# Moving a depthwise convolution wholly to VectorE and spreading it and its norm through the attention heads, with the first modulation computed feature tile by feature tile

## The chip, the cores and the metric

The kernel runs on one core of a Trainium2 chip. The metric is the device time of one execution in microseconds (us). A core has engines that run side by side, each with its own queue of instructions: TensorE (PE, matrix products; its weight loads are listed as PEld), VectorE (DVE), ScalarE (ACT), GpSimd (POOL), and SyncE (SP), which here only issues DMAs. They wait for each other on semaphores.

## What is computed

Two transformer blocks on 256 tokens of 1024 features, all in float32. The first block is the one that the change touches:

```python
m = silu(c) @ w_mod + b_mod                     # 6 vectors of 1024: shift, scale, gate, twice
hx = rms_norm(x, g) * (1 + sc1) + sh1           # and the same for ctx, with c_ctx
q, k, v, u, g = split(hx @ w_in)                # 8 query heads, 2 key/value heads of 128
attn = softmax(q k^T / sqrt(128)) v             # 512 keys: ctx and x; q, k are normed and rotated
a, b = split(u)                                 # 512 + 512
h = depthwise_conv(a * sigmoid(b), 31 taps) + bias
y_b = silu(layer_norm(h)) @ w_conv_out
x = x + g1 * ((sigmoid(g_a) * (attn @ w_attn_out) + sigmoid(g_b) * y_b) @ w_out)
x = x + g2 * conv_glu_ffn(rms_norm(x) * (1 + sc2) + sh2)
```

The second block (two gated FFNs, two kinds of attention, a gated embedding) follows. The modulation vectors sh1 and sc1 are needed ahead of every product with hx; g1, sh2, sc2 and g2 only after the attention.

## The kernel before, in words

**Weights and products.** All weights are streamed once from HBM in chunks of 1 MiB (128 partitions x 2048 floats) into four buffers `raw`, by SP in the order of the list `STREAM`. A chunk of a product is then split in two: ACT rounds it (`whi<-raw`, L1031), DVE takes the rest (`wlo<-raw,whi`, L1386), and PE makes three products for each tile instead of one (`product`). There are four buffers of either half too. The features x are split the same way (`x_hi`, `x_lo`). A product whose stationary operand is x has 512 columns (L573 to L575; stages q, kv, w_out, down), one whose stationary operand is the weight has 256 (L576 to L578; stages u, g, attention out, conv out, up). A 1 MiB chunk of the second kind is 48 products and fills one of PSUM's four banks `acc` (`tiles_stage`). A `tiles_stage` waits for `lo_done`, so for both halves.

**Modulation.** `w_mod` needs no split: PE multiplies its raw chunk k, the rows of feature tile k, by silu(c) (L645, four matmuls of 512 columns in four column groups of the array, `mod_chunk`). Each of the three blocks modA, modB, modC covers 2048 outputs, so all eight chunks have to be summed before any output exists. `mod_turn` (L653) then turns the row into columns, DVE adds the bias (L1453), and for modA DVE and ACT apply it to the transposed features (`x_lo`, `x_hi`).

**Order of the stages** is written out by hand in each engine's block and in `STAGES` (which also gives PSUM banks): modA (8 chunks), q (4), u (4), kv (2), g0, g1, then eight heads, in which the remaining g chunks and modB, modC are placed (`MOD_PER_HEAD` = 1, 1, 2, 2, 2, 2, 3, 3), then attention out (4 chunks), conv out (2), w_out (4) and the FFN. In a head PE runs `scores(h)` (L715), `values(h - 1)` (L736), modulation chunks, a g chunk and `prob_transposes(h)` (L724). DVE finds the negated maximum of the scores (L1552), ACT exponentiates (L1153) and scales (L1157), then copies the transposed probabilities (L1169).

**The convolution** has 31 taps on 4 tiles of 128 channels x 256 tokens. Two channel tiles are done on GpSimd (`conv_taps`, L474 and L475: a multiply and an add of 512 columns for each tap, from the end of the kv stage on), the other two on DVE inside the heads (`conv_tap`, L1544, one instruction for a tap and tile, 8 in a head). The layer norm comes after the last head: `ln_mean` (L763), DVE subtracts (L1586), ACT squares (L1176), `ln_var` (L771) inside the attention out stage, GpSimd's root, `ln_broadcast` (L779), DVE scales (L1613), ACT's silu (L1184) and split (L1188), DVE's `cvt_lo` (L1592). The conv out product comes after attention out, then the merge of the branches (L1598, L1623, L1626, L1629).

## Time and profile before

| | us |
|---|---|
| median of 3 runs | 1117.77 (1116.77 to 1118.16) |
| the profiled execution: time | 1119.8 |
| the profiled execution: span of the trace | 1118.0 |
| PE busy | 1018.6 (91%), 6592 matmuls |
| DVE / ACT / POOL busy | 619.9 (55%) / 504.0 (45%) / 136.4 (12%) |
| DMA | 189.02 MB, 169 GB/s on average; 118498 packets, 95312 of them under 2 KB |
| chain that ended last | PE 78%, DVE 13%, ACT 3%, DMA 3% |

All times below are from the span's start. PE is busy nearly all the time from 333 us on (the FFNs and the second block); the change touches only what comes before, except for the layout of the weights in HBM. PE's busy time counts a matmul from start to end and neighbours overlap, so a stretch of matmuls is better read by the distance of their starts.

### The profile page before, as it was taken

The page shows a single profiled execution, that of the slowest core. Times are in us where ns is not written, and L with a number is a line of the kernel's source. Part 1 is how long each engine was busy: PE and PEld are TensorE (multiplying, and loading weights), DVE is VectorE, ACT ScalarE, POOL GpSimd, SP SyncE. Part 2 cuts the span into 40 slices and gives each one's busy share as a digit, 9 for nine tenths or more (in the row PEclk, how much of TensorE's full clock was granted, in tenths as well). Part 3 has the DMA queues.
Part 4 walks back from the last instruction along what each step waited for, and adds up shares of the span by engine and source line. Part 5 has one row for each costly group of instructions (what it writes and reads, how often), then busy time and mean ns, then how long its engine had stood idle before and what let it go on. Part 6 is the DMA issues. An engine that isn't in the chain of part 4 may idle for free.

```text
span 1118.0 us, 15950 instructions
## 1 busy us (share of the span) xinstructions
PE 1018.6 (91%) x6592; PEld 901.3 (81%) x6592; DVE 619.9 (55%) x686; ACT 504.0 (45%) x628; POOL 136.4 (12%) x157
## 2 busy tenths in 40 slices
PE   4699997689989999997999999979999799999997
PEld 1498775458869999985999998778977599999886
DVE  0585387836787666545554544463345664545445
ACT  2563244335435666432544443347633354444343
POOL 3120699500000000001000000010000100000000
PEclk9699998898989999999899999989975899999999
DMA  9755055376555556463555547534421366554621
GB/s 355 278 166 210 3 194 181 113 264 206 188 169 191 187 174 201 174 203 113 188 178 184 171 143 236 178 123 151 148 79 56 115 188 188 183 183 167 213 81 38
DMA packets 118498, 189.02 MB, mean 169 GB/s; under 512 B 3024, under 2 KB 95312, under 8 KB 115376
## 3 DMA queue, kind: packets, MB, share of 16 engines
q1 hardware_dynamic: 116624, 181.61, 48.2%
q0 software_dynamic: 1136, 4.06, 1.2%
q10 hardware_dynamic: 688, 2.63, 0.6%
q8 instruction: 38, 0.62, 0.2%
q14 instruction: 12, 0.10, 0.0%
HBM read 187.24 MB, written 1.05 MB: 168 GB/s over the span
## 4 chain that ended last, share of the span: by engine, by line
PE 78%; DVE 13%; ACT 3%; DMA 3%; issue 1%; POOL 1%; SPq 0%; DVEq 0%; POOLq 0%; ACTq 0%
PE acc L576 15%; PE acc L577 15%; PE acc L578 15%; PE acc L573 9%; PE acc L575 9%; PE acc L574 9%; DVE XN L1544 4%; DVE wlo L1386 3%; DMA raw<-in_w_mod 2%; ACT whi L1031 1%; PE acc L645 1%; DMA raw<-in_w_attn_out 1%; DVE XN L1400 1%; PE tp L662 1%; ACT FULL L1153 1%
## 5 line engine op out<-in xcount | busy, mean ns | idle before, releaser
L1386 DVE TENSOR_TENSOR wlo<-raw,whi 128x2048 fp32r<-128x2048 f32 x148 | 340.1, 2312 | 221.0 <-ACT whi L1031 220.7
L576 PE MATMUL acc<-x_hi,whi 128*128 128x256 f32 x1376 | 395.0, 287 | 3.8 <-DVE x_lo L1424 2.0
L577 PE MATMUL acc<-x_lo,whi 128*128 128x256 f32 x1376 | 392.7, 285 | 0.0
L578 PE MATMUL acc<-x_hi,wlo 128*128 128x256 f32 x1376 | 392.5, 285 | 0.0
L1031 ACT CAST whi<-raw 128x2048 fp32r<-128x2048 f32 x148 | 280.3, 1910 | 184.5 <-PE acc L575 90.9
L576 PEld LDWEIGHTS acc<-x_hi,whi 128*128 128x128 f32 x1376 | 267.6, 194 | 11.6 <-issue 10.0
L577 PEld LDWEIGHTS acc<-x_lo,whi 128*128 128x128 f32 x1376 | 267.7, 195 | 0.0
L578 PEld LDWEIGHTS acc<-x_hi,wlo 128*128 128x128 f32 x1376 | 267.6, 194 | 0.0
L573 PE MATMUL acc<-whi,h_hi 128*128 128x512 f32 x264 | 103.1, 391 | 0.0
L574 PE MATMUL acc<-wlo,h_hi 128*128 128x512 f32 x264 | 102.7, 389 | 0.0
L575 PE MATMUL acc<-whi,h_lo 128*128 128x512 f32 x264 | 102.7, 389 | 0.0
L573 PE MATMUL acc<-whi,x_hi 128*128 128x512 f32 x176 | 72.3, 411 | 12.3 <-DVE x_lo L1431 5.8
L575 PE MATMUL acc<-whi,x_lo 128*128 128x512 f32 x176 | 71.2, 405 | 0.0
L574 PE MATMUL acc<-wlo,x_hi 128*128 128x512 f32 x176 | 71.1, 404 | 0.0
L574 PEld LDWEIGHTS acc<-wlo,h_hi 128*128 128x128 f32 x264 | 49.6, 188 | 10.5 <-issue 0.2
L573 PEld LDWEIGHTS acc<-whi,h_hi 128*128 128x128 f32 x264 | 49.6, 188 | 10.4 <-issue 0.2
L575 PEld LDWEIGHTS acc<-whi,h_lo 128*128 128x128 f32 x264 | 49.6, 188 | 10.2
L517 POOL TENSOR_SCALAR small<-small 128x1 f32<-128x1 f32 x8 | 3.5, 438 | 423.8 <-ACT XN L1261 399.6
L437 POOL TENSOR_SCALAR small<-small 128x1 f32<-128x1 f32 (+2 forms) x19 | 7.4, 390 | 384.7 <-ACT XN L1250 194.2
L573 PEld LDWEIGHTS acc<-whi,x_hi 128*128 128x128 f32 x176 | 34.8, 198 | 22.0 <-issue 10.0
L1544 DVE SCALAR_TENSOR_TENSOR XN<-conv_x,vt,XN 128x256 f32<-128x256 f32 x60 | 51.6, 930 | 0.0
L645 PE MATMUL acc<-raw,sct 128*32 128x512 f32 x192 | 29.6, 727 | 24.0 <-DMA raw<-in_w_mod 20.9
(238 smaller groups left out, 1118.5 us busy)
## 6 DMA issues: line engine op xcount, KB each, us to landing
raw<-in_w_in SPq DMA_DIRECT2D x30, 1024.0 KB, 5.5
raw<-in_w_mod SPq DMA_DIRECT2D x24, 1024.0 KB, 7.9
raw<-in_w_up SPq DMA_DIRECT2D x22, 1024.0 KB, 5.1
raw<-in_w_ffn_gate SPq DMA_DIRECT2D x22, 1024.0 KB, 5.3
raw<-in_w_ffn_up SPq DMA_DIRECT2D x22, 1024.0 KB, 5.4
raw<-in_w_ffn_down SPq DMA_DIRECT2D x22, 1024.0 KB, 5.0
raw<-in_w_down SPq DMA_DIRECT2D x11, 1024.0 KB, 5.0
raw<-in_w_out SPq DMA_DIRECT2D x8, 1024.0 KB, 5.0
```

Of the source, the lines that this page charges most:

```text
L573: pe.matmul(out, xh, wh, start=start, stop=False)
L574: pe.matmul(out, xh, wl, start=False, stop=False)
L575: return pe.matmul(out, xl, wh, start=False, stop=stop)
L576: pe.matmul(out, wh, xh, start=start, stop=False)
L577: pe.matmul(out, wh, xl, start=False, stop=False)
L578: return pe.matmul(out, wl, xh, start=False, stop=stop)
L645: mm = pe.matmul(acc[32 * b:32 * b + 32, MOD_BANK, :], sct[:, k, :], raw[c % NR][:, b * MW:(b + 1) * MW], start=(k == 0), stop=(k == KD - 1))
L662: mm = pe.transpose(tp[:, k // 2, (k % 2) * T + t * P:(k % 2) * T + (t + 1) * P], source[:, t, k * P:(k + 1) * P], ident)
L1031: act.copy(whi[si_slot][:, :], raw[raw_slot][:, :]).then_inc(s["hi_done"], 1)
L1153: act.activation(half(FULL, t), tp[:, t, :], ACT.Exp, bias=nmax[:, t:t + 1], accum_out=psum_[:, t:t + 1]).then_inc(s["p_exp"], 1)
L1386: dve.tensor_tensor(wlo[slot][:, :], raw[raw_slot][:, :], whi[slot][:, :], ALU.subtract)\
L1544: dve.scalar_tensor_tensor(at, conv_x[:, k, i:i + T], w, at, ALU.mult, ALU.add)\
```

## The change

1. **Modulation A by feature tiles.** `modA` leaves `STREAM`. The host lays its weights out so that chunk k holds, for all 1024 inputs, the shift and the scale of feature tile k. It goes into one of four buffers `early` of its own. `first_mod(k)` makes eight matmuls of 256 columns instead of four of 512, `first_turn(k)` sums the column groups and turns them, DVE's `first_row`, `first_out`, `first_lo` and ACT's `first_hi` finish feature tile k. The q stage now takes chunks of two feature tiles by all 1024 columns, and PE runs `q_tile(k - 2)` between `first_mod(k)` and `first_turn(k)`. x is loaded ahead of everything but the vectors, on SP; only 138 of the 1034 columns of constants are loaded first. The context's norm and transposes move behind the u stage.
2. **Convolution on DVE only**, 124 instructions of 256 columns: 16 after the first half of u, 2, 7, 8 and 12 behind the key units, 17 in each head until done (in head 4). GpSimd's `conv_taps` is gone.
3. **Norm and half the product inside the heads.** `ln_mean` and `ln_var` in head 5, `ln_broadcast`, silu and split in head 6; `convout0` takes the place of a g chunk in head 7, `convout1` follows `values(7)`; attention out comes after, and the merge goes column block by column block with it.
4. **Even heads.** Two modulation chunks and one g chunk in each; g1 moves from ahead of the heads into head 0. In head 0 the modulation chunks come ahead of the scores, in head 4 the g chunk comes ahead of them.
5. **One array `stream`** in HBM: the host packs each chunk as 128 rows of 8 KB, where it was read in pieces of 1, 2 or 4 KB (modulation: 8 KB).

The core of the diff:

```diff
-MOD_PER_HEAD = (1, 1, 2, 2, 2, 2, 3, 3)
-
-
-STAGES = [("modA", KD, 1), ("q", 4, 4), ("u", 4, 4), ("kv", 2, 4), ("g0", 1, 1), ("g1", 1, 1)]
+MOD_PER_HEAD = (2, 2, 2, 2, 2, 2, 2, 2)
...
-    if _h + 2 < NH:
-        STAGES.append((f"g{_h + 2}", 1, 1))
-STAGES.append(("pv7", 0, 1))
+        _turn.append((f"{_block}.{_k}", 1, int(_k == KD - 1)))
+    _big = (f"g{_h + 1}", 1, 1) if _h + 1 < NH else ("convout0", 1, 2)
+
+    STAGES += [_big] + _turn if _h == 4 else _turn + [_big]
+    if _h == 5:
+        STAGES.append(("ln_var", 0, 1))
+STAGES += [("pv7", 0, 1), ("convout1", 1, 2)]
 ROTATE3 = {f"g{_h}" for _h in range(NH)} | {f"pv{_h}" for _h in range(NH)}
-STAGES += [(f"attnout{_j}", 1, 1) for _j in range(4)]
-STAGES += [("convout", 2, 4), ("g1b", 0, 2), ("wout", 4, 4), ("up0", 22, 22), ("down0", 11, 4)]
...
+            def ring(c):
+                slot_free(c)
+                sp.dma_start(raw[c % NR][:, :], stream[c, :, :]).then_inc(landed[c % NR], 16)
+
+            def first_block(k):
+                if k >= 4:
+                    sp.wait_ge(s["moda_ps"], k - 3)
...
+            for t in range(TT):
+                sp.dma_start(X[:, t, :], a["x"][t * P:(t + 1) * P, :]).then_inc(s[f"x_in{t}"], 16)
+            first_block(0)
+            ring(POS["q", 0])
+            first_block(1)
+            first_block(2)
+            ring(POS["q", 1])
+            first_block(3)
+            first_block(4)
+            ring(POS["q", 2])
+            first_block(5)
+            first_block(6)
+            ring(POS["q", 3])
+            first_block(7)
+            ring(POS["u", 0])
+            sp.dma_start(consts[:, C_FIRST:C_END], a["consts"][:, C_FIRST:C_END]).then_inc(s["rest_in"], 16)
+            ring(POS["u", 1])
+            sp.dma_start(CTX, a["ctx"].rearrange("(t p) d -> p t d", p=P)).then_inc(s["ctx_in"], 16)
+            for name, j in STREAM[POS["u", 2]:]:
                 c0 = POS[name, 0]
                 if not name.startswith("up"):
-                    c = POS[name, j]
-                    slot_free(c)
-                    w = src[name][j]
-                    sp.dma_start(raw[c % NR][:, :].rearrange("p (k n) -> p k n", k=w.shape[1]), w)\
-                        .then_inc(landed[c % NR], 16)
+                    ring(POS[name, j])
                     continue
...
-            def conv_taps(k0, k1, first):
-
-                out = conv[:, k0:k1, :]
-                for i in range(first, TAPS):
-                    w = per_channel(vt[:, 1, KC * i + k0:KC * i + k1])
-                    x = conv_x[:, k0:k1, i:i + T]
-                    if i == 0:
-                        chain(pool.tensor_tensor(out, x, w, ALU.mult))
-                        chain(pool.tensor_tensor(out, out, per_channel(vec("conv_dw_b", k1 - k0, k0)), ALU.add))
-                        continue
-                    term = half(XN, i % 2)[:, 0:(k1 - k0) * T].rearrange("p (k n) -> p k n", k=k1 - k0)
-                    chain(pool.tensor_tensor(term, x, w, ALU.mult))
-                    ins = pool.tensor_tensor(out, out, term, ALU.add)
-                    if i < TAPS - 1:
-                        chain(ins)
-                ins.then_inc(s["conv_out"], 1)
-
-            conv_taps(KC - KP, KC, 0)
...
+            def first_mod(k):
+
+                pe.wait_ge(early_in[k % 4], 16 * (k // 4 + 1))
+                if k >= 2:
+                    pe.wait_ge(s["mod_row"], k - 1)
+                for j in range(2):
+                    for b in range(MB):
+                        r = MB * j + b
+                        mm = pe.matmul(tp[32 * b:32 * b + 32, k % 2, 0:T], sct[:, r, :],
+                                       early[k % 4][:, r * T:(r + 1) * T], start=(j == 0), stop=(j == 1))
+                mm.then_inc(s["moda_ps"], 1)
+
+            def first_turn(k):
+
+                pe.wait_ge(s["mod_row"], k + 1)
+                for q in range(2):
+                    mm = pe.matmul(tp[:, 2, 4 * k + 2 * q:4 * k + 2 * q + 2],
+                                   modrow[:, (k % 2) * T + q * P:(k % 2) * T + (q + 1) * P], pick_sum,
+                                   start=True, stop=True)
+                mm.then_inc(s["mod_ps"], 1)
...
+            def q_tile(k):
+
+                chunk_ready(SPLIT["q"] + k // 2)
+                pe.wait_ge(s["x0_lo"], k + 1)
+                if k == 0:
+                    pe.wait_ge(s["xt_in"], 4)
+                w = [r[(SPLIT["q"] + k // 2) % NR][:, :].rearrange("p (k n) -> p k n", k=2) for r in (whi, wlo)]
+                for b in range(2):
+                    for t in range(TT):
+                        mm = product(accb(ACC["q"] + 2 * b + t), xhi[:, k, t * P:(t + 1) * P],
...
+            x_transposes(0)
+            first_mod(0)
+            x_transposes(1)
+            first_turn(0)
+            first_mod(1)
+            first_turn(1)
+            for k in range(2, KD - 1):
+                first_mod(k)
+                q_tile(k - 2)
+                first_turn(k)
+            first_mod(KD - 1)
+            first_turn(KD - 1)
+            q_tile(5)
+            q_tile(6)
+            q_tile(7)
 
             def rope_transposes(u):
...
             for h in range(NH):
+                if h == 0:
+                    mod_chunks(0)
                 scores(h)
                 if h:
                     values(h - 1)
+                if h == 5:
+                    ln_mean()
+                if h == 6:
+                    ln_broadcast()
                 if h == MOD_DONE["modB"] + 1:
                     mod_turn("modB")
-                for _, block, k in [m for m in MOD_AT if m[0] == h]:
-                    mod_chunk(block, k, POS[f"{block}.{k}", 0])
-                if h + 2 < NH:
-                    tiles_stage(SPLIT[f"g{h + 2}"], ACC[f"g{h + 2}"])
+                    tiles_stage(SPLIT[f"g{h + 1}"], ACC[f"g{h + 1}"])
+                    mod_chunks(h)
+                elif h + 1 < NH:
+                    if h:
+                        mod_chunks(h)
+                    tiles_stage(SPLIT[f"g{h + 1}"], ACC[f"g{h + 1}"])
+                else:
+                    mod_chunks(h)
+                    conv_products(0)
+                if h == 5:
+                    ln_var()
                 prob_transposes(h)
+            mod_turn("modC")
             values(NH - 1)
-            mod_turn("modC")
-
-
-            sq = QT[:, 0:4, :]
...
+                if h == 5:
+                    act.wait_ge(s["ln_c"], 1)
+                    act.activation(QT[:, 0:4, :], conv, ACT.Square).then_inc(s["ln_sq"], 1)
+                if h == 6:
+                    act.wait_ge(s["ln_n"], 1)
+                    for k in range(KC):
+                        ins = act.activation(QT[:, k, :], conv[:, k, :], ACT.Silu, scale=vec("conv_ln_g", 1, k),
+                                             bias=vec("conv_ln_b", 1, k))
+                    ins.then_inc(s["ln_y"], 1)
+                    act.wait_ge(s["ln_y"], 1)
+                    act.copy(cvt_hi[:, :, :], QT[:, 0:4, :]).then_inc(s["ln_hi"], 1)
+                if h == 7:
...
+            def first_row(k):
+
+                dve.wait_ge(s["moda_ps"], k + 1)
+                dve.tensor_copy(modrow[:, (k % 2) * T:(k % 2 + 1) * T], tp[:, k % 2, 0:T]).then_inc(s["mod_row"], 1)
...
+            def first_lo(k):
+
+                dve.wait_ge(s["x0_hi"], k + 1)
+                dve.wait_ge(s["affine1"], k + 1)
+                dve.scalar_tensor_tensor(FULL[:, k, :], FULL[:, k, :], gainA[:, 0, k:k + 1], xhi[:, k, :], ALU.mult,
+                                         ALU.subtract).then_inc(s["shift_dve"], 1)
+                n_shift[0] += 1
+                dve.wait_ge(s["shift_dve"], n_shift[0])
+                dve.tensor_scalar(xlo[:, k, :], FULL[:, k, :], modv[:, k, 0:1], None, ALU.add).then_inc(s["x0_lo"], 1)
+
...
+            def conv_taps(count):
+
+                for n in range(n_tap[0], min(n_tap[0] + count, TAPS * KC)):
+                    pair, i, k = n // (2 * TAPS), n % (2 * TAPS) // 2, n % 2
...
+                        dve.wait_ge(s["conv_dve"], n - 1)
+                        dve.scalar_tensor_tensor(at, conv_x[:, k, i:i + T], w, at, ALU.mult, ALU.add)\
+                            .then_inc(s["conv_dve"], 1)
+                n_tap[0] = min(n_tap[0] + count, TAPS * KC)
+
...
+                if h == 6:
                     dve.wait_ge(s["ln_r"], 1)
                     for t in range(TT):
                         ins = dve.tensor_scalar(half(XN, 0)[:, t * P:(t + 1) * P], ident, lnv[:, t:t + 1], -1.0,
                                                 ALU.mult, ALU.mult)
                     ins.then_inc(s["ln_diag"], 1)
-                elif j == 1:
-                    dve.wait_ge(s["ln_bc"], 1)
-                    dve.tensor_tensor(cent, cent, over_tiles(tp[:, 2, 0:T]), ALU.mult).then_inc(s["ln_n"], 1)
-            splits_to(SPLIT["convout"] + 2)
-            splits_to(SPLIT["wout"] + 2)
-
-            dve.wait_ge(s["g_sig"], 2)
-            dve.wait_ge(s["ya_done"], 4)
+                conv_taps(3)
+                for t in range(TT):
+                    dve.wait_ge(s["p_exp"], TT * h + t + 1)
+                    dve.reciprocal(prec[:, t:t + 1], psum_[:, t:t + 1]).then_inc(s["p_rec"], 1)
+
+                if h:
+                    pv_lo(h - 1)
+                if h == MOD_DONE["modB"] + 1:
+                    mod_out("modB")
+                if h == 5:
+                    bank_ready(ACC["ln_mean"])
+                    dve.tensor_tensor(conv, conv, over_tiles(accb(ACC["ln_mean"])[:, 0:T]), ALU.subtract)\
+                        .then_inc(s["ln_c"], 1)
+                conv_taps(6)
+                splits_to(SPLIT["g2"] + h + 1)
+                conv_taps(8)
+                if h == MOD_DONE["modB"]:
+                    mod_row("modB")
+                if h == 5:
+                    bank_ready(ACC["ln_var"])
+                    dve.tensor_copy(lnv, accb(ACC["ln_var"])[:, 0:TT]).then_inc(s["ln_ve"], 1)
+                if h == 6:
+                    bank_ready(ACC["ln_bc"])
+                    dve.wait_ge(s["ln_c"], 1)
+                    dve.tensor_tensor(conv, conv, over_tiles(accb(ACC["ln_bc"])[:, 0:T]), ALU.mult)\
...
+    stream = np.empty((len(STREAM), P, CH), np.float32)
+    for c, (name, j) in enumerate(STREAM):
+        w, r, k, c0, n = SOURCE[name][j]
+        stream[c] = arrays[w][r * P:(r + k) * P, c0:c0 + n].reshape(k, P, n).transpose(1, 0, 2).reshape(P, CH)
+    first = arrays["w_mod"][:, 0:2 * D].reshape(KD, P, 2, KD, P).transpose(3, 1, 0, 2, 4)
+    arrays["early"] = np.ascontiguousarray(first).reshape(KD, P, CH)
```

How the order moves. PE at the start of the program, before (L645 is `mod_chunk`, L662 the transposes of x, L653 `mod_turn`, then the products of q):

```order
L645 MATMUL acc<-raw,sct 32x512 x16
L662 MATMUL tp<-consts,XN 128x128 x16
L645 MATMUL acc<-raw,sct 32x512 x16
L653 MATMUL acc<-consts,modrow 128x8 x4
L573 MATMUL acc<-whi,x_hi 128x512
L574 MATMUL acc<-wlo,x_hi 128x512
L575 MATMUL acc<-whi,x_lo 128x512
L573 MATMUL acc<-whi,x_hi 128x512
```

and of the change (L723 the transposes of x, L706 `first_mod`, L714 `first_turn`, L594 to L596 the products of q):

```order
L723 MATMUL acc<-consts,XN 128x128 x8
L706 MATMUL tp<-early,sct 32x256 x8
L723 MATMUL acc<-consts,XN 128x128 x8
L714 MATMUL tp<-consts,modrow 128x2 x2
L706 MATMUL tp<-early,sct 32x256 x8
L714 MATMUL tp<-consts,modrow 128x2 x2
L706 MATMUL tp<-early,sct 32x256 x8
L594 MATMUL acc<-whi,x_hi 128x512
L595 MATMUL acc<-wlo,x_hi 128x512
L596 MATMUL acc<-whi,x_lo 128x512
```

The first q product now comes after three modulation chunks instead of after eight, and after both transposes of x; another modulation chunk and its turn follow each twelve products.

DVE in one head (head 2), before (L1552 maximum, L1556 reciprocal, L1527 `pv_lo`, L1386 split, L1544 convolution):

```order
L1552 TENSOR_REDUCE small<-tp 128x1 x2
L1556 RECIPROCAL small<-small 128x1 x2
L1527 TENSOR_TENSOR side_lo<-acc,side_hi 128x256
L1386 TENSOR_TENSOR wlo<-raw,whi 128x2048
L1544 SCALAR_TENSOR_TENSOR XN<-conv_x,vt,XN 128x256 x8
```

and of the change (the same in L1730, L1741, L1714, L1506, L1690):

```order
L1730 TENSOR_REDUCE small<-tp 128x1 x2
L1690 SCALAR_TENSOR_TENSOR XN<-conv_x,vt,XN 128x256 x3
L1741 RECIPROCAL small<-small 128x1 x2
L1714 TENSOR_TENSOR side_lo<-acc,side_hi 128x256
L1690 SCALAR_TENSOR_TENSOR XN<-conv_x,vt,XN 128x256 x6
L1506 TENSOR_TENSOR wlo<-raw,whi 128x2048
L1690 SCALAR_TENSOR_TENSOR XN<-conv_x,vt,XN 128x256 x8
```

Eight convolution instructions became 17, and the split moved from ahead of them to between the ninth and the tenth.

ACT from head 6 to head 7 of the change (L1272 exp, L1276 scale, L1259 `pv_hi`, L1131 split, L1289 silu, L1293 split of its result, L1263 `g_out`, L1301 copy of the transposed probabilities):

```order
L1272 ACTIVATE FULL,small<-tp,small 128x512 x2
L1276 ACTIVATE FULL<-FULL,small 128x512 x2
L1259 CAST side_hi<-acc 128x256
L1131 CAST whi<-raw 128x2048
L1289 ACT_TABLE_LOAD
L1289 ACTIVATE QT<-XN,vt 128x256 x4
L1293 CAST cvt_hi<-QT 128x1024
L1263 COPY G<-acc 128x512
L1301 COPY FULL<-tp 128x4x128 x2
L1272 ACT_TABLE_LOAD
L1272 ACTIVATE FULL,small<-tp,small 128x512 x2
L1276 ACTIVATE FULL<-FULL,small 128x512 x2
```

The silu and its split, which came after all heads before, now stand between head 6's weight split and its `g_out`, with a table load ahead of the silu and another ahead of the next exp.

## Rows read from the trace of the kernel before

**Rows 1.** Windows: length, busy PE, PEld, DVE, ACT, POOL, PEclk, DMA share, GB/s.

```profile
0.00:12.00 12.00, 0.00 (x0) 0.01 (x1) 0.27 (x1) 1.60 (x3) 2.43 (x11) 1.00 0.85 270
12.00:36.00 24.00, 14.52 (x80) 3.23 (x80) 0.53 (x1) 6.27 (x7) 6.01 (x12) 0.93 1.02 413
...
144.00:222.00 78.00, 61.74 (x362) 45.03 (x360) 63.38 (x68) 29.26 (x55) 64.06 (x49) 0.89 0.44 156
```

**Rows 2.** Waits of TensorE, 0 to 335 us: in total, times, longest.

```profile
PE acc L645 <- DMA raw<-in_w_mod: 20.9, 7, 12.0
PE tp L724 <- ACT FULL L1157: 12.4, 3, 4.4
PE acc L573 <- DVE x_lo L1431: 5.8, 1, 5.8
```

**Rows 3.** Timeline of TensorE to the end of q: start, us, what [idle before].

```profile
12.02 1.94 PE L645 MATMUL acc<-raw,sct 128*32 128x512 f32 x8 [12.02 <-DMA raw<-in_w_mod]
...
25.80 1.06 PE L645 MATMUL acc<-raw,sct 128*32 128x512 f32 x8 [0.32 <-DMA raw<-in_w_mod]
...
33.46 1.94 PE L645 MATMUL acc<-raw,sct 128*32 128x512 f32 x8 [4.11 <-DMA raw<-in_w_mod]
43.93 0.77 PE L573 MATMUL acc<-whi,x_hi 128*128 128x512 f32 x1 [5.85 <-DVE x_lo L1431]
...
59.26 0.48 PE L573 MATMUL acc<-whi,x_hi 128*128 128x512 f32 x1
...
70.01 0.40 PE L575 MATMUL acc<-whi,x_lo 128*128 128x512 f32 x1
```

**Rows 4.** Timeline of TensorE, heads 0 and 1, and to the end of w_out.

```profile
135.68 1.98 PE L715 MATMUL tp<-KT,QT 128*128 128x512 f32 x4 [0.46 <-ACT KT L1114]
...
138.59 0.39 PE L576 MATMUL acc<-x_hi,whi 128*128 128x256 f32 x1
...
144.44 1.04 PE L724 MATMUL tp<-consts,FULL 128*128 128x128 f32 x8
145.31 1.88 PE L715 MATMUL tp<-KT,QT 128*128 128x512 f32 x4
147.03 1.89 PE L736 MATMUL acc<-FULL,V 128*128 128x256 f32 x8
...
252.43 3.75 PE L736 MATMUL acc<-FULL,V 128*128 128x256 f32 x8 [3.86 <-ACT FULL L1169]
...
323.11 0.39 PE L575 MATMUL acc<-whi,x_lo 128*128 128x512 f32 x1
```

**Rows 5.** Timeline of VectorE in heads 3 and 4.

```profile
189.77 1.28 DVE L1552 TENSOR_REDUCE small<-tp 128x1 f32<-128x512 f32 x2
...
195.25 2.58 DVE L1386 TENSOR_TENSOR wlo<-raw,whi 128x2048 fp32r<-128x2048 f32 x1 [1.37 <-ACT whi L1031]
197.75 10.49 DVE L1544 SCALAR_TENSOR_TENSOR XN<-conv_x,vt,XN 128x256 f32<-128x256 f32 x8
...
215.84 3.25 DVE L1544 SCALAR_TENSOR_TENSOR XN<-conv_x,vt,XN 128x256 f32<-128x256 f32 x8
```

**Rows 6.** Timeline of GpSimd: the root for the first q unit.

```profile
64.11 1.02 POOL L433 TENSOR_TENSOR small<-small 128x4 f32<-128x4 f32 x1
```

**Rows 7.** The page, DMA issues: median us to landing at the end.

```profile
raw<-in_w_mod SPq DMA_DIRECT2D x24, 1024.0 KB, 7.9
...
raw<-in_w_out SPq DMA_DIRECT2D x8, 1024.0 KB, 5.0
```

**Rows 8.** Timeline of ScalarE, norm after the heads.

```profile
263.05 1.06 ACT L1176 ACTIVATE QT<-QT 128x1024 f32<-128x1024 f32 x1 [4.66 <-DVE QT L1586]
264.12 1.28 ACT L1179 ACT_TABLE_LOAD   x1
265.42 1.92 ACT L1179 ACTIVATE G<-G 128x2048 f32<-128x2048 f32 x1
...
276.79 2.08 ACT L1184 ACTIVATE QT<-QT,vt 128x256 f32<-128x256 f32 x4 [2.75 <-DVE QT L1613]
```

618 lines of the change are left out of this document (341 added, 277 removed).

## The prediction

> **What bounds the kernel now.** I read the windows first, then TensorE's waits, then its timeline and the queues it waits for. From 333 us on TensorE is busy nearly throughout, and the change leaves those stages alone, so the question is what happens ahead of 324 us, where the last w_out product ends (323.11 plus 0.40, a few records missing) [rows 4]. The windows show three different limits there. Up to 36 us it is DMA: 270 GB/s in the first 12 us, then 413 GB/s at a share of 1.02 [rows 1]. TensorE waits 20.9 us for modulation chunks and then 5.8 us for VectorE's x_lo [rows 2]; the last modA chunk is used at 33.46, the first q product starts at 43.93 and the last at 70.01 [rows 3]. From 144 to 222 us, heads 1 to 4, TensorE is busy 61.7 of 78 us and VectorE 63.4, beside 64.1 of GpSimd [rows 1]. TensorE's waits there are for probabilities (12.4 us) [rows 2], and those are late since VectorE takes the maxima only after its taps. Eight taps take 10.49 us while GpSimd convolves and 3.25 us in head 4, where it has finished [rows 5]: 1.31 against 0.41 us for one and the same instruction.
>
> TensorE's clock shows in the rows too. A modulation chunk takes 1.94 us after idle time and 1.06 later [rows 3]: 1.2 and 2.4 GHz. At the higher level 48 products of 512 columns run from 59.26 to 70.01, so 0.229 each; a chunk of 48 products of 256 columns takes 144.44 - 138.59 = 5.85, transposes 0.9, scores 1.7, values about 1.8 [rows 4].
>
> **Start to end of q: 70.4 to 54.5, -15.9.** Through the last early chunk the queue now carries 12 MiB of chunks, 1 of x and 0.4 MB besides, 14.0 MB. By the rates of [rows 1], 3.2 MB are in by 12 us and the rest takes 26: it lands at 38, some 5 later than modA did, since the four q chunks now travel in between. But then only one chunk, its turn and three q tiles remain: 1.1 + 1.2 + 3 x 12 x 0.229 = 10.5, an end at 49. That is the lower bound. TensorE's own work is longer: it starts when x is normed, about 10.5 (1.25 MB ahead in the queue, then two squares and a scale of 1024 columns, each about the 1.06 of [rows 8], and GpSimd's root). Transposes 2, eight chunks 8.5, eight turns 4 with their waits, 96 products 22: 36.5, so 47 at full clock. The low clock doubles what runs in the first 12 us or so, as it did before up to chunk four [rows 3]: +5. VectorE's chain (copy, bias, gain, x_lo, weight split of 2.3 ahead of the first q tile) adds about 2.5. I take 54.5. If the clock stayed low through the tiles between the chunks, five tiles would cost 2.7 more each.
>
> **End of q to the first scores: 65.3 to 63.2, -2.1.** g1 leaves this stretch (-5.9), and about 3.8 of small waits with it. Added: the context's 16 transposes 1.9; the first two modulation chunks, now ahead of the scores, 2.1; the first u chunk no longer has a split to wait for but a bank, freed after squares, a root of 1.02 [rows 6] and VectorE's multiply, 1.6; q's last copy ahead of the context's transposes 0.9; the kv stage's second chunk behind 16 taps (16 x 0.41 = 6.5, mostly beside u), 1.0; the fifth key unit 1.0 and small items. The taps here, 45 x 0.41 = 18, cost nothing else, since VectorE is half idle in kv and g0; without that cover they would cost up to 18.
>
> **Heads: 120.5 to 111.6, -8.9.** Before, 135.68 to 256.2 with six g chunks. Now TensorE's head is scores 1.7, values 1.8, two modulation chunks 1.9, a g chunk 5.85 and transposes 0.9, 12.2 in all. VectorE's round is maxima 1.28, three taps 1.2, reciprocals 0.3, a wait of about 1.7 for ScalarE's scalings, pv_lo 0.4, six taps 2.4, split 2.3 [rows 5], eight taps 3.25: 12.9. A third round runs through DMA. SP issues in order, and the first modulation chunk of the next head waits for the split of the g chunk four before it; that split now ends 10.6 after the head's start. A landing takes 5.0 for an unhurried chunk and 7.9 in a queue [rows 7], and the pair's second chunk is needed; so 10.6 + 7.8 + 1 + 5.9 + 0.9 = 26.2 for two heads, 13.1 each. I take 13.2 for heads 2 and 3. Head 0 has neither values nor chunks behind its scores, 8.6; head 1 waits 3.3 for a chunk whose load was not issued until head 0's split, 15.6. Head 4 has the turn of modB, 14.2. Head 5 has no taps left but the mean and the variance (1.8 each, four matmuls of 256 columns as in values), 15.8; head 6 the broadcast, 12.9. Head 7 waits for its values: ScalarE's silu (2.08) with a table load of 1.28 and the 1.05 cast stand ahead of g_out and of the copies of head 6's probabilities. Counted from head 6's start, the norm's product is ready at 11.8, the copies at 18.1, and TensorE would want them at 15.4: 2.7, head 7 is 15.0. With the turn of modC and values(7), 3.1, the sum is 111.6 (8.6 + 15.6 + 26.4 + 14.2 + 15.8 + 12.9 + 15.0 + 3.1).
>
> The table load took 1.28, between an end at 264.11 and a start at 265.42 [rows 8]. The Trainium skill (ScalarE: Activation LUTs, "What ACT_TABLE_LOAD costs") gives about 2.66 us for a switch, the load plus a drain of about 1.38. Two added switches lie on this path (silu, then exp again), and by the page the sum would be 2.8 worse; no drain shows in this trace's row, so the row decides.
>
> **After the heads: 67.8 to 53.7, -14.1.** One of two conv chunks 5.9, four of attention out 23.4, the gate's broadcast 1.9, 96 w_out products 22.0, half a microsecond of waits. Gone: the other conv chunk (in head 7), mean, variance and broadcast, the wait of 3.86 and half-speed values behind the late attention weight [rows 4], and the stalls at the merge, whose column blocks now follow their own attention out chunk. VectorE and ScalarE each need about 4.5 for a chunk's split and block against 5.85.
>
> **The rest: 0.** The stream in rows of 8 KB loads faster, but from 333 us on no chunk is waited for; a gain could only come where one was.
>
> **Sum.** -15.9 - 2.1 - 8.9 - 14.1 = -41.0 against the profiled span of 1118.0, so 1077.0. The profiled execution took 1119.8, 2.0 above the median of 1117.77; the same step from the median gives 1076.8. I say **1077**.
>
> **Rivals.**
> - *Every round hides*: heads at TensorE's 12.2, no wait in heads 1 and 7, q's end at the DMA bound plus little (51). 3 + 3.3 + 2.7 + 3.5 = -12.5: about 1065. For it speaks that steady work keeps the clock up; against, that three rounds of nearly equal length hardly all miss each other. 0.12.
> - *The clock stays low in the interleaved start*: its pieces are short and each waits for VectorE, as modulation chunks did in the first 20 us [rows 3]. Five tiles at +2.7: +13.5, about 1091. Against: after idle time the q stage ran up within 6 us of its start. 0.13.
> - *The load round decides the heads*: with both landings of a pair at 7.9 and 10.5 [rows 7] it becomes 14.5 a head and each wait lowers the clock, so that half of TensorE's waiting comes again as slow work: (1.3 + 0.7) x 7 = +14, about 1091. 0.15.
> - *Taps stay slow: slower than before.* If the 1.31 us [rows 5] were the tap's own price in the heads (its three SBUF operands, beside ScalarE and DMA) and not GpSimd's doing, VectorE's round would be 28 us for 4.6 heads, +69, and the 16 taps ahead of kv's second chunk +14: about 1160. It decides from 0.84 us a tap on: 95 taps on the path x 0.43 = 41. Against it stand the three groups of eight in 3.25 with GpSimd idle, in head 4 [rows 5] and two after. 0.03.
> - The change does what it says: queues and waits agree with it, so none for that.
>
> **Chances.** Forecast (1070 to 1085) 0.54, the rivals as above, 0.03 for something unseen, a third of it on the slow side. A measurement here can tell about 0.2%, 2.2 us, from no change. Faster by more than that: 0.95; within: 0.01; slower: 0.04. The range 1063 to 1096 takes in the first three rivals with the bounds of q's end (49 to 68) and leaves out the last.
>
> **What would show it.** In the changed trace: q's last product near 54 and full speed from about 25; scores(0) near 118; taps at 0.41 throughout, and GpSimd silent; heads 2 and 3 at 13 us from scores to scores; one wait of 3 us for a modulation chunk in head 1 and one for probabilities in head 7; w_out's end at 283, and from there to the end of the span the same 794 us as before. I am wrong if q ends after 60, if taps take over 0.6, if heads 2 and 3 take over 15, or if the stretch from w_out's end on differs by over 3.

## The result, and the profile after

The changed kernel takes **1087.46 us** (median of 4 runs, 1086.28 to 1087.97) against 1117.76 of the kernel before in the same comparison: ratio 0.9725, 95% interval 0.9711 to 0.9739. It is faster by 30.3 us, where 41 were forecast; 1087.5 lies inside the range of 1063 to 1096. The profiled execution has a span of 1085.9 for 1118.0. That is 32.1 less and not 30.3, since the profiled execution of the kernel before took 2.0 us more than its median. Cut at the borders of the prediction's steps, the spans compare so:

| stretch | before | forecast | after | off by |
|---|---|---|---|---|
| start to end of q | 70.4 | 54.5 | 63.3 | +8.8 |
| end of q to first scores | 65.3 | 63.2 | 60.8 | -2.4 |
| heads | 120.5 | 111.6 | 109.9 | -1.7 |
| after the heads, to w_out's end | 67.8 | 53.7 | 51.7 | -2.0 |
| the rest | 794.0 | 794.0 | 800.3 | +6.3 |

Two stretches are missed, the first and the last, and together they make more than the whole error. The page of the changed kernel:

```profile
span 1085.9 us, 16198 instructions
...
PE 1014.5 (93%) x6680; PEld 904.1 (83%) x6680; DVE 618.9 (57%) x772; ACT 507.3 (47%) x629; POOL 53.2 (5%) x95
...
L594 PE MATMUL acc<-whi,h_hi 128*128 128x512 f32 x264 | 104.8, 397 | 0.0
L595 PE MATMUL acc<-wlo,h_hi 128*128 128x512 f32 x264 | 104.4, 395 | 0.0
...
L1690 DVE SCALAR_TENSOR_TENSOR XN<-conv_x,vt,XN 128x256 f32<-128x256 f32 x120 | 49.1, 477 | 0.0
```

GpSimd is nearly silent (5%). The L594 and L595 rows are the products of the three down stages with the hidden values h_hi; in the profile before, their mean was 391 and 389 ns. The change touches nothing in those stages. TensorE's four longest entries up to the end of the heads (234 us), with the total, the number of waits and the longest one:

```profile
PE acc L723 <- ACT XN L1170: 11.5, 1, 11.5
PE tp L714 <- DVE modrow L1575: 5.7, 2, 4.7
PE acc L671 <- DMA raw<-in_stream: 5.3, 3, 2.6
PE acc L594 <- DVE wlo L1506: 3.4, 2, 2.9
```

(Norms further on cost TensorE another 25.5 us, as they did before with 26.3.) The 20.9 us for chunks of w_mod and the 12.4 for probabilities [rows 2] are gone. In their place stand 11.5 until x is normed, 4.7 for one modulation row, 5.3 for three chunks of the stream and 2.9 for the first q split.

**Where the start is lost.** TensorE's timeline from the last modulation chunk to the last q products:

```profile
45.31 0.51 PE L714 MATMUL tp<-consts,modrow 128*128 128x2 f32 x4
45.75 1.07 PE L706 MATMUL tp<-early,sct 128*32 128x256 f32 x16
51.56 1.02 PE L714 MATMUL tp<-consts,modrow 128*128 128x2 f32 x4 [4.74 <-DVE modrow L1575]
52.44 0.77 PE L594 MATMUL acc<-whi,x_hi 128*128 128x512 f32 x1
53.01 0.63 PE L595 MATMUL acc<-wlo,x_hi 128*128 128x512 f32 x1
...
57.69 0.40 PE L594 MATMUL acc<-whi,x_hi 128*128 128x512 f32 x1
...
62.93 0.39 PE L596 MATMUL acc<-whi,x_lo 128*128 128x512 f32 x1
```

The last chunk is multiplied at 46.8, its turn starts at 51.56. Behind that wait the turn takes 1.02 for 0.51 and the first twelve products start 0.43 apart for 0.23 (53.01 to 57.69): the lower of the clock's two levels. VectorE's queue in that gap:

```profile
48.88 2.29 DVE L1506 TENSOR_TENSOR wlo<-raw,whi 128x2048 fp32r<-128x2048 f32 x1 [2.46 <-ACT whi L1131]
51.09 0.42 DVE L1575 COPY modrow<-tp 128x256 f32<-128x256 f32 x1
```

The row's 0.42 us copy stands behind the split of the fourth q chunk, and the split behind ScalarE's half of it (46.96 to 48.84). The row was ready at 46.8.

**Where head 1 loses.** Scores start at 124.07, 132.51, 151.38, 163.51, 177.02, 189.99, 205.57 and 218.13; heads 2 and 3 take 12.1 and 13.5 (head 3 with one wait of 1.2 for a modulation chunk), head 1 takes 18.9:

```profile
132.51 1.88 PE L801 MATMUL tp<-KT,QT 128*128 128x512 f32 x4
134.22 1.89 PE L822 MATMUL acc<-FULL,V 128*128 128x256 f32 x8
138.73 1.14 PE L671 MATMUL acc<-raw,sct 128*32 128x512 f32 x8 [2.62 <-DMA raw<-in_stream]
141.41 1.93 PE L671 MATMUL acc<-raw,sct 128*32 128x512 f32 x8 [1.53 <-DMA raw<-in_stream]
150.51 1.03 PE L810 MATMUL tp<-consts,FULL 128*128 128x128 f32 x8
```

Two waits for modulation chunks, and behind them the low clock: the second chunk takes 1.93 for 1.07 and the g chunk 7.2 for the 5.85 of [rows 4]. Taps are fast in all heads, as VectorE's timeline of head 1 shows, where before eight of them took 10.49 us beside GpSimd [rows 5]:

```profile
141.49 2.45 DVE L1690 SCALAR_TENSOR_TENSOR XN<-conv_x,vt,XN 128x256 f32<-128x256 f32 x6
143.86 2.28 DVE L1506 TENSOR_TENSOR wlo<-raw,whi 128x2048 fp32r<-128x2048 f32 x1
146.06 3.25 DVE L1690 SCALAR_TENSOR_TENSOR XN<-conv_x,vt,XN 128x256 f32<-128x256 f32 x8
```

### The profile page after: what moved, and what is told of

Its sections match the earlier page's. It is cut to its first block, busy times and chain, and to the rows that moved or that the text cites. A ratio compares the mean times of both kernels' runs of the same rounds, so it can differ in the third digit from the quotient of the medians.

```text
span 1085.9 us, 16198 instructions
## 1 busy us (share of the span) xinstructions
PE 1014.5 (93%) x6680; PEld 904.1 (83%) x6680; DVE 618.9 (57%) x772; ACT 507.3 (47%) x629; POOL 53.2 (5%) x95
## 4 chain that ended last, share of the span: by engine, by line
PE 86%; DVE 5%; ACT 3%; issue 1%; DMA 1%; POOL 1%; DVEq 0%; SPq 0%; POOLq 0%; ACTq 0%
PE acc L597 16%; PE acc L598 16%; PE acc L599 16%; PE acc L594 9%; PE acc L595 9%; PE acc L596 9%; DMA raw<-in_stream 1%; PE acc L671 1%; ACT whi L1131 1%; DVE wlo L1506 1%; PE tp L801 1%; DVE XN L1520 1%; PE acc L822 1%; DVE XN L1897 1%; PE tp L1026 1%
## 5 line engine op out<-in xcount | busy, mean ns | idle before, releaser
L1506 DVE TENSOR_TENSOR wlo<-raw,whi 128x2048 fp32r<-128x2048 f32 x148 | 337.7, 2292 | 222.2 <-ACT whi L1131 221.7
L1131 ACT CAST whi<-raw 128x2048 fp32r<-128x2048 f32 x148 | 280.5, 1907 | 175.9 <-PE acc L596 97.4
L597 PEld LDWEIGHTS acc<-x_hi,whi 128*128 128x128 f32 x1376 | 269.3, 196 | 12.5 <-issue 12.1
L594 PE MATMUL acc<-whi,h_hi 128*128 128x512 f32 x264 | 104.8, 397 | 0.0
L595 PE MATMUL acc<-wlo,h_hi 128*128 128x512 f32 x264 | 104.4, 395 | 0.0
L596 PE MATMUL acc<-whi,h_lo 128*128 128x512 f32 x264 | 104.4, 395 | 0.0
L594 PE MATMUL acc<-whi,x_hi 128*128 128x512 f32 x176 | 72.3, 411 | 5.7 <-DVE wlo L1506 3.4
L595 PE MATMUL acc<-wlo,x_hi 128*128 128x512 f32 x176 | 70.5, 401 | 0.0
L596 PE MATMUL acc<-whi,x_lo 128*128 128x512 f32 x176 | 70.5, 401 | 0.0
L595 PEld LDWEIGHTS acc<-wlo,h_hi 128*128 128x128 f32 x264 | 49.6, 188 | 12.2 <-issue 0.2
L594 PEld LDWEIGHTS acc<-whi,h_hi 128*128 128x128 f32 x264 | 49.6, 188 | 12.1 <-issue 0.2
L596 PEld LDWEIGHTS acc<-whi,h_lo 128*128 128x128 f32 x264 | 49.6, 188 | 11.9
L1690 DVE SCALAR_TENSOR_TENSOR XN<-conv_x,vt,XN 128x256 f32<-128x256 f32 x120 | 49.1, 477 | 0.0
L594 PEld LDWEIGHTS acc<-whi,x_hi 128*128 128x128 f32 x176 | 34.5, 196 | 15.8 <-DVE wlo L1506 5.1
L1852 DVE TENSOR_TENSOR FULL<-acc,XN 128x512 f32<-128x512 f32 x33 | 22.8, 691 | 39.8 <-PE acc L599 39.8
L1346 ACT ACTIVATE XN<-acc 128x512 f32<-128x512 f32 x22 | 13.1, 597 | 61.2 <-PE acc L599 61.2
L596 PEld LDWEIGHTS acc<-whi,x_lo 128*128 128x128 f32 x176 | 34.2, 194 | 7.6
## 6 DMA issues: line engine op xcount, KB each, us to landing
early<-in_early SPq DMA_DIRECT2D x8, 1024.0 KB, 14.1
G<-in_ctx SPq DMA_DIRECT2D x1, 1024.0 KB, 14.7
```

Of the source, the lines that this page charges most:

```text
L594: pe.matmul(out, xh, wh, start=start, stop=False)
L595: pe.matmul(out, xh, wl, start=False, stop=False)
L596: return pe.matmul(out, xl, wh, start=False, stop=stop)
L597: pe.matmul(out, wh, xh, start=start, stop=False)
L1131: act.copy(whi[si_slot][:, :], raw[raw_slot][:, :]).then_inc(s["hi_done"], 1)
L1346: act.activation(half(XN, 2 + q), accb(g), ACT.Silu).then_inc(s["glu_act"], 1)
```

## The experiments

Times are medians; a ratio is to the kernel before on the same chip, with its 95% interval. The changed kernel alone stands at 1087.5.

### One copy ahead of the split

```diff
+            first_row(7)
             splits_to(4)
-            first_row(7)
```

> The changed kernel with two lines of VectorE's queue exchanged: the copy of the last modulation row out of its bank (first_row(7)) goes ahead of the split of the fourth q chunk. Queue theory: that row waited 4.7 us behind a split which itself waited for ScalarE's half, and the wait threw TensorE back to the low clock, so the last 36 q products took 10.9 us for 8.2. Then q's last product ends near 56.5 for 63.3, and the time falls by 6 to 7 us, to 1081. Rival, the start is bound by loads or by VectorE's whole chain there: the split is late instead and the last tiles wait for it; q ends at 61 to 63, the time stays within 2 us of 1087.5.

**Measured: 1083.56, ratio 0.9684 (0.9667 to 0.9701), 3.9 less.** TensorE, around the row:

```profile
48.04 1.07 PE L706 MATMUL tp<-early,sct 128*32 128x256 f32 x16
49.66 0.61 PE L714 MATMUL tp<-consts,modrow 128*128 128x2 f32 x4 [0.55 <-DVE modrow L1575]
...
54.20 0.47 PE L594 MATMUL acc<-whi,x_hi 128*128 128x512 f32 x1 [1.09 <-DVE x_lo L1598]
```

The wait is 0.55 for 4.74, the turn 0.61 for 1.02, the last 36 products 8.7 for 10.9, and the last q product ends at 59.9 instead of 63.3, though the first operand was ready 1.7 us later in this execution (TensorE's first wait is 13.2, not 11.5). From the first product to q's end it is 46.7 for 51.8, so 5.1 less. With the start of the changed kernel q would have ended at 58.2, and not at the 56.5 that was expected: 1.1 of the wait comes back as a wait for x_lo, and the first q tile, here at the low clock to its end, took 0.9 longer (25.16 to 30.43, for 23.81 to 28.14). The queue theory holds in kind; the time fell by 3.9 and not by 6 to 7.

### g2's split ahead of the heads

The line is added twice, for ScalarE behind its last key unit and for VectorE behind that unit's taps:

```diff
+            splits_to(SPLIT["g2"] + 1)
```

> The changed kernel with the split of g chunk 2 ahead of the heads on both ScalarE and VectorE, instead of inside head 0, so that the slot for the modulation chunk of head 1 comes free earlier. Load theory: head 1's two waits for modulation chunks (2.6 and 1.5 us) and the low clock behind them (its g chunk took 7.4 us for 5.85) go: head 1 is 14 us instead of 18.9, the time falls by 4 to 5 us, to 1083. Rival, the slot is not what is late but the DMA queue ahead of it (the landing takes as long however early it is issued), or the split ahead of head 0 delays the first maxima by its 2.3 us: the waits move to head 2 or to head 0 and the time stays within 2 us of 1087.5.

**Measured: 1080.66, ratio 0.9663 (0.9646 to 0.9679), 6.8 less.**

```profile
134.71 1.89 PE L822 MATMUL acc<-FULL,V 128*128 128x256 f32 x8
136.53 1.93 PE L671 MATMUL acc<-raw,sct 128*32 128x512 f32 x16
144.23 1.03 PE L810 MATMUL tp<-consts,FULL 128*128 128x128 f32 x8
145.10 1.88 PE L801 MATMUL tp<-KT,QT 128*128 128x512 f32 x4
...
149.23 1.06 PE L671 MATMUL acc<-raw,sct 128*32 128x512 f32 x8 [0.53 <-DMA raw<-in_stream]
151.72 1.07 PE L671 MATMUL acc<-raw,sct 128*32 128x512 f32 x8 [1.42 <-DMA raw<-in_stream]
```

Head 1 is 12.1, without a wait and at full clock; head 2 takes a part back (14.3 for 12.1, with two waits of 0.5 and 1.4), as the rival said of the place but not of the size. w_out ends 4.9 earlier. The other 1.9 of the 6.8 were not located: the rest of the span is 799.0 for 800.3, and in the traces with h_hi at the same address as here it scatters from 798.3 to 800.4.

### TensorE's start without the interleaving

```diff
+            for k in range(1, KD):
-            first_mod(1)
-            first_turn(1)
-            for k in range(2, KD - 1):
                 first_mod(k)
                 first_turn(k)
-                q_tile(k - 2)
...
+            for k in range(KD):
+                q_tile(k)
-            q_tile(5)
-            q_tile(6)
-            q_tile(7)
```

> The changed kernel with the interleaving of its start taken back on TensorE alone: all eight modulation chunks and their turns first, then the eight q tiles; loads, VectorE and ScalarE as they are. Theory, the interleaving is what brings q forward: the tiles, 2.9 to 3.0 us each, then stand behind the last turn near 40 to 51, q ends at 66 to 75, the time rises by 4 to 10 us, to about 1094. Rival, the start is bound by loads and VectorE, and TensorE runs the same tiles at full clock in one piece: q ends within 2 us of 63.3 and the time stays at 1087.

**Measured: 1093.40, ratio 0.9780 (0.9753 to 0.9807), 5.9 more.** q ends at 70.2, just where it ended before the change (70.4). The last chunks and the first product:

```profile
38.87 1.01 PE L714 MATMUL tp<-consts,modrow 128*128 128x2 f32 x4 [0.70 <-DVE modrow L1569]
39.81 1.93 PE L706 MATMUL tp<-early,sct 128*32 128x256 f32 x16
45.42 1.01 PE L714 MATMUL tp<-consts,modrow 128*128 128x2 f32 x4 [3.68 <-DVE modrow L1569]
46.30 0.77 PE L594 MATMUL acc<-whi,x_hi 128*128 128x512 f32 x1
```

So with VectorE's queue as it is, the whole gain of the start, 7 us, hangs on TensorE's order. Without tiles in between four turns wait 0.55 to 0.71 for their rows, and every chunk from 25.8 to 41.7 takes 1.93, the lower level; with them it is 1.07 from 28.6 on. Two turns wait much longer, 3.99 (at 24.86) and 3.68, again behind a split in VectorE's queue. That queue was written for the interleaved order; a serial start with a queue of its own was not tried, so the price of the serial order as such stays open.

### The convolution on VectorE, alone

The kernel before, with all 124 taps on VectorE, 16 in each head, and none on GpSimd:

```diff
-KP = 2
+KP = 0
...
-            conv_taps(KC - KP, KC, 0)
...
-                pe.wait_ge(s["conv_out"], 1)
```

> The kernel before with one part of the change alone: VectorE does all 124 taps inside the heads, 16 a head, and GpSimd none; product, norm, modulation and start stay where they were. Interference theory: each tap falls from 1.31 to 0.41 us, 8 in 10.5 us become 16 in 6.5, VectorE's round in heads 0 to 3 is 4 us shorter and in the later heads 3.3 longer, while TensorE waits in the first ones alone (12.4 us for probabilities); conv_out is no longer waited for. Time 1105 to 1110. Rival, the taps are dear in the heads for their own operands: 16 a head at 1.31 is 21 us, 10.5 more in each of 8 heads, time above 1180.

**Measured: 1115.71, ratio 0.9970 (0.9953 to 0.9988): 3 us less,** where one theory had 8 to 13 less and the other over 60 more. VectorE in its rounds of heads 2 and 4 (TensorE is a head further by then):

```profile
172.63 6.42 DVE L1518 SCALAR_TENSOR_TENSOR XN<-conv_x,vt,XN 128x256 f32<-128x256 f32 x16
...
205.35 6.41 DVE L1518 SCALAR_TENSOR_TENSOR XN<-conv_x,vt,XN 128x256 f32<-128x256 f32 x16
211.69 0.68 DVE L1414 COPY modrow<-acc 128x512 f32<-128x512 f32 x1
```

and TensorE in head 5:

```profile
212.43 1.87 PE L628 MATMUL acc<-consts,modrow 128*128 128x8 f32 x8 [4.06 <-DVE modrow L1414]
216.61 3.64 PE L620 MATMUL acc<-raw,sct 128*32 128x512 f32 x16 [2.31 <-DVE mod L1427]
```

The tap's price is settled: 16 in 6.42, 0.40 each, in head 2 of the old order, where before eight took 10.49 as in head 3 [rows 5]. Nothing else was edited, so the difference is GpSimd's doing. VectorE's maxima, which read PSUM, take 1.28 with and without it (189.77 in [rows 5]; 164.24 here). The Trainium skill (GPSIMD Engine Reference, "1. Specifications") has the SBUF interfaces shared between GpSimd and VectorE, with contention for VectorE instructions that have two SBUF inputs. A tap is one, and the trace agrees: 1.31 beside GpSimd's convolution, 0.40 without it. What happens inside is not shown. Heads 2, 3 and 4 fall from 19.1, 18.4 and 18.6 to 14.2, 14.7 and 16.5. But head 5 rises from 21.3 to 28.3: the turn of modB waits for a 0.68 us copy behind the 16 taps. By the start of the seventh head 6.4 us are won, 2.6 of them ahead of the first scores, and at w_out's end 1.6 are left. By these rows the order of VectorE's queue decides what the faster tap is worth; no run moved that copy alone.

### The layout of the stream, alone

The kernel before, its chunks laid out one behind the other in DRAM by the host; order, engines and waits unchanged.

```diff
-                    w = src[name][j]
-                    sp.dma_start(raw[c % NR][:, :].rearrange("p (k n) -> p k n", k=w.shape[1]), w)\
+                    sp.dma_start(raw[c % NR][:, :], stream[c, :, :])\
```

> The kernel before with one part of the change alone: the host lays the weight chunks out in DRAM one behind the other in the order of their loads, each partition's 8 KB in one piece. Order, engines and waits are those of before. Layout theory: faster loads change little where nothing waits for them, up to 36 us they bring the last modulation chunk forward by the ratio of the rates (413 to about 420 GB/s, 0.5 us), and if the layout is what slows the down stages' products (397 ns for 391) the time is 1117.8 + 5 = 1123. Rival: layout has no part in that, and the time is 1116 to 1118.

**Measured: 1115.80, ratio 0.9976 (0.9958 to 0.9994); down products 391 ns.** The layout alone is worth some 3 us (0.7 to 4.7 by the interval), and it does not slow the down stages.

### Why the down stages are slower

The stretch behind w_out had grown by 6.3 us. In the kernel before, the page has for these products

```profile
L573 PE MATMUL acc<-whi,h_hi 128*128 128x512 f32 x264 | 103.1, 391 | 0.0
...
L574 PE MATMUL acc<-wlo,side_hi 128*128 128x512 f32 x16 | 6.3, 395 | 0.0
```

and for h_hi 397 in the changed one. Products with h_hi and h_lo (792 in all, three groups of 264) start 0.2333 us apart for 0.2268: 5.1 us. Stages with x_hi kept their pitch, which speaks against the clock and the loads. What the change does to h_hi is to move it: the constants grew by 8 bytes a partition, and all tiles behind them shifted (by 32 bytes, as is told below). (The expectation of the first run counts 2376 products; 792 is right.)

```diff
+        consts = sb("consts", [P, 1048])
-        consts = sb("consts", [P, C_END])
```

> The changed kernel with its table of constants made 14 floats longer per partition (1048 for 1034), so that all tiles behind it in SBUF, those of the feed-forward's hidden values among them, start again at the multiple of 64 bytes that they had before the change. Nothing reads the added floats. Address theory: the 512-column products of the three down stages return from a pitch of 0.2333 us to 0.2268, about 5 us in 2376 products; the stretch from w_out's end to the end of the span is 795 instead of 800, the time 1082.5. Rival, the slower stretch comes from the stream's new order and layout in DRAM (DMA writes into SBUF beside the products) or from the clock: pitch 0.233, stretch 800, time 1087.5.

**Measured: 1086.92, ratio 0.9718 (0.9702 to 0.9734); 397 ns.** No gain.

```diff
+        small = sb("small", [P, 158])
-        small = sb("small", [P, 160])
```

> The changed kernel with its tile of small values 2 floats shorter (158 for 160, the last ones unused), so that every tile behind it, the feed-forward's hidden values among them, lies at the very address that it had before the change. The run with 1048 constants put them 64 bytes further and the pitch stayed at 397 ns a product against 391 (mean of the record), so a multiple of 64 does not matter; this leaves the address as a whole. Address theory: 391 ns, stretch behind w_out 795, time 1082.5. Rival (stream layout or another cause): 397 ns, 800, 1087.

**Measured: 1087.14, ratio 0.9719 (0.9694 to 0.9744); 397 ns.** Taken by itself this speaks against addresses. Its mirror in the kernel before speaks for them:

```diff
+        small = sb("small", [P, 162])
-        small = sb("small", [P, 160])
```

> The kernel before with its tile of small values 2 floats longer, which shifts all tiles behind it by 8 bytes a partition, as the change did. Address theory: down products 397 ns for 391, time about 1123. Rival: 391 ns, time 1117.8 within 1.

**Measured: 1123.42, ratio 1.0042 (1.0030 to 1.0054); 397 ns.** One number in the source of the old kernel, nothing else, and it has the new kernel's products and 799.1 behind w_out (a first form of this mirror, with the old constants 2 floats longer, gave no result, since that tile then no longer matched the array that is loaded into it):

```profile
L573 PE MATMUL acc<-whi,h_hi 128*128 128x512 f32 x264 | 104.8, 397 | 0.0
...
L574 PE MATMUL acc<-wlo,side_hi 128*128 128x512 f32 x16 | 6.2, 389 | 0.0
```

The second row moves the other way: the same shift took the kv stage's products with side_hi from 395 to 389 ns. Why the run before it said nothing is told by the rounding: a tile's size goes up to the next 32 bytes, so 158 floats had moved nothing, and 162 moved everything behind them by 32. The same in the changed kernel, with a size that does reach the old address:

```diff
+        small = sb("small", [P, 152])
-        small = sb("small", [P, 160])
```

> The changed kernel with its tile of small values 8 floats shorter (152 for 160, the last ones unused). The program rounds each tile up to 32 bytes; so the constants' 8 added bytes had moved the hidden values h_hi from byte 177792 of a partition to 177824, and the two earlier attempts put them at 177856 (constants of 1048) and again at 177824 (small of 158, which rounds up to the same), not at 177792 as their texts assumed. Here they are at 177792 for the first time. Address theory, as the kernel before with all shifted by 32 bytes bears it out (397 ns for 391, time up by 4.7): 391 ns, stretch behind w_out 795, time 1082.5. Rival, the cause in the changed kernel is another one that looks the same: 397 ns, 1087.

**Measured: 1081.79, ratio 0.9674 (0.9647 to 0.9701), 5.7 less; the rest is 794.7.**

```profile
L594 PE MATMUL acc<-whi,h_hi 128*128 128x512 f32 x264 | 103.1, 391 | 0.0
L595 PE MATMUL acc<-wlo,h_hi 128*128 128x512 f32 x264 | 102.7, 389 | 0.0
```

### All three together

The row first, g2's split early, and a third address for h_hi:

```diff
+        consts = sb("consts", [P, 1064])
-        consts = sb("consts", [P, C_END])
...
+            splits_to(SPLIT["g2"] + 1)
...
+            first_row(7)
             splits_to(4)
-            first_row(7)
```

> The changed kernel with the three mends together: the last modulation row ahead of the split in VectorE's queue, the split of g chunk 2 ahead of the heads, and the constants 30 floats longer (1064), which puts h_hi at byte 177920, 128 bytes from where it lay before. Multiple-of-128 theory: 391 ns a down product. Apart the first gave -3.9 and the second -6.8; with -5 for the address the sum is -15.7 from 1087.5, 1072. Rival, only the old address itself is good (or another multiple than 128 counts): 397 ns and 1077.

**Measured: 1075.15, ratio 0.9614 (0.9589 to 0.9639); 396 ns.** It is 12.3 less than the changed kernel, where the first two mends make 10.7 apart, so they add up at least; 128 bytes further is no good address:

```profile
L594 PE MATMUL acc<-whi,h_hi 128*128 128x512 f32 x264 | 104.5, 396 | 0.0
```

The same two mends at the old address (this edit and the next are given against the run with all three together):

```diff
+        small = sb("small", [P, 152])
-        small = sb("small", [P, 160])
-        consts = sb("consts", [P, 1064])
+        consts = sb("consts", [P, C_END])
```

> The three mends together again, but with the small tile 8 floats shorter, so that h_hi lies at byte 177792, its address in the kernel before. With h_hi at byte 177920, 128 further, a down product was 396 ns and the time 1075.2. Address theory: 391 ns, 4 to 5 us less behind w_out, 1070.5. Rival: with head 1 and the start mended the down stages meet other traffic and the pitch stays at 396, 1075.

**Measured: 1070.97, ratio 0.9585 (0.9550 to 0.9621); 391 ns.** It is 16.5 less than the changed kernel, and the three apart make 3.9 + 6.8 + 5.7 = 16.4. And 256 bytes behind that address:

```diff
+        consts = sb("consts", [P, 1096])
-        consts = sb("consts", [P, 1064])
```

> The first two mends with h_hi 256 bytes behind its old place, at byte 178048. Offsets of 32, 64 and 128 bytes were all slow (397, 397 and 396 ns). The moving operands (whi, wlo) and the old h_hi all lie 128 bytes above a multiple of 512. Residue theory: if what counts is the distance between stationary and moving operand modulo 256, it is 391 ns and 1070.5 here. Rival (modulo 512, or the one address alone): 396 ns and 1075.

**Measured: 1070.45, ratio 0.9584 (0.9547 to 0.9620).**

```profile
L594 PE MATMUL acc<-whi,h_hi 128*128 128x512 f32 x264 | 103.1, 391 | 0.0
```

Both versions beat the changed kernel by 16 to 17 us and the kernel before by 46. Between them there is no difference that these runs can tell.

## Why the prediction was right or wrong

**The mechanism and most stretches were right; the time was missed by 10.7 us.** Of these 8.9 lie in the trace (1085.9 for 1077.0); the other 1.8 come from reading the steps in an execution of the kernel before that was itself 2.0 slower than its median. Taps at 0.41 throughout, GpSimd silent, heads 2 and 3 at 12.1 and 13.5 for 13.2, head 0 at 8.4 for 8.6, head 5 at 15.6 for 15.8, head 6 at 12.6 for 12.9, and 51.7 behind the heads for 53.7. Two of the four marks that were to say "I am wrong" came up, however: q ended after 60, and the rest differed by over 3.

**Start to end of q, the term "VectorE's chain adds about 2.5": mis-sized, and by its form.** The terms were summed as amounts of work. What cost time was one place in a queue: the 0.42 us copy behind a 2.29 us split, itself 2.46 late for ScalarE. The exchange of the two showed 5.1 of the 8.8, half of that because the turn and the products behind it no longer run at the low clock. Towards the other 3.7 go a first product 1.0 later than assumed (11.5 for 10.5), and a first q tile that waits 2.9 for its split and runs 4.5 for 3.0; they were not tried apart. That the split was named as a term ("2.3 ahead of the first q tile") did not help: the fourth split, ahead of the last row, was not looked for. The low clock came as the rival feared, but for seven products of the first q tile and for the twelve behind the last turn, not for five tiles.

**End of q to scores, -2.1 for -4.5 measured.** The recorded terms do not add up to the -2.1: -5.9 and -3.8 gone, and 1.9, 2.1, 1.6, 0.9, 1.0 and 1.0 added, make -1.2, so it is 3.3 off by its own terms. The waits were 1.6, 0.7 and 0.5 for the 1.6, 0.9 and 1.0 of u's bank, the context and the kv chunk: 0.7. The larger part is a term that the sum left out. In the kernel before, the longest of the waits that were counted as gone was followed by eight products 0.43 apart, and the granted clock of the stretch was 0.97, where it is 1.00 now:

```profile
100.42 0.50 PE L573 MATMUL acc<-whi,x_hi 128*128 128x512 f32 x1 [2.07 <-DVE wlo L1386]
...
101.57 0.63 PE L573 MATMUL acc<-whi,x_hi 128*128 128x512 f32 x1
```

That is some 1.6 us of slow work, gone with the wait. The last 1.0 was not located.

**Heads: the sum within 1.7, by luck: errors of opposite sign.** Head 1 was put at 15.6 with one wait of 3.3; it had two, 2.6 and 1.5, and 2.2 of low clock behind them, 18.9. The cause was named rightly, a load that is not issued until head 0's split, and moving that split took the waits away. What the sum left out is that a wait is paid again in slow work: 2.2 us behind 4.1 of waiting here, and 2.6 behind 4.7 at the start. The rival of the load round had this right ("half of TensorE's waiting comes again as slow work"). Against the 3.3 of head 1 stand head 7 with what follows it, put at 18.1 with 2.7 of waiting, which took 15.8 with 0.5; head 4, 13.0 for 14.2; and heads 2 and 3, 25.6 for 26.4. The table load that was charged to the path lay in ScalarE's own wait, and so cost nothing:

```profile
212.30 1.28 ACT L1289 ACT_TABLE_LOAD   x1
215.77 2.08 ACT L1289 ACTIVATE QT<-XN,vt 128x256 f32<-128x256 f32 x4 [2.19 <-DVE XN L1762]
...
220.40 1.28 ACT L1272 ACT_TABLE_LOAD   x1
221.70 0.69 ACT L1272 ACTIVATE FULL<-tp,small 128x512 f32<-128x512 f32 x1
```

The second pair shows what one costs where nothing hides it: 1.28 and no drain behind it, the work starts 0.02 us after its end. The Trainium skill (ScalarE: Activation LUTs, "What ACT_TABLE_LOAD costs") has 2.66; the row decides again for 1.28, as the sum had it.

**After the heads, -14.1 for -16.1 measured: right**, with the conv chunk, the half-speed values and the stalls at the merge gone, as listed. The 2.0 by which it was still better were not located.

**"The rest: 0" was wrong, +6.3.** It rested on "the change leaves those stages alone". It did so in code, order and waits, and the new layout of the loads did not matter (391 ns in the old kernel with it), but the addresses were not left alone. Moving h_hi back gave 5.6 of the 6.3 in the trace (794.7 for 800.3) and 5.7 in the median; the reverse move in the old kernel cost 4.7. The row and the address alone, as each was measured, would bring the gain to 30.3 + 3.9 + 5.7 = 39.9 of the 41 forecast, if they add; no run has these two alone. With g2's split moved too it was measured, 46.

**The rivals.** "Every round hides" did not come, for the waits of the start and head 1; "the load round decides the heads" came true in head 1 alone (the landing of 10.5 that it takes from [rows 7] does not stand there; the rows have 7.9 and 5.0); "taps stay slow" is refuted at 0.41 and 0.40 in two kernels. The faster side was right by the interval.

## What to carry to other kernels

Where an in-order queue serves the bottleneck engine, list it row by row around each hand-over and ask what stands ahead of the shortest instruction that somebody waits for: a 0.4 us copy behind a split cost 5 us here, and another behind 16 taps stands where most of what faster taps had won was lost. Where a wait of TensorE is followed by rows at half speed, charge it one and a half times (2.2 on top of 4.1, 2.6 on top of 4.7 here), and fill the gaps between dependent pieces with independent products. When the size of any tile changes, compare the addresses of the operands that TensorE reads before calling the untouched stages free.
